# Rows of the first tile in ticks of their own, and every third of its first 48 added by TensorE

## The reference

```
q = (xf @ w_query).reshape(T, 8, 2, 128)
s = einsum('thcd,hckd->thck', q, sub_keys)
top_s, top_i = lax.top_k(s, 16)                 # of 128 keys, twice per head
cand_s, cand_i = sums and numbers of the 16 x 16 pairs
best_s, pos = lax.top_k(cand_s, 16)             # 16 experts of 16384 per head
gates = softmax(best_s)
a = gelu(einsum('cd,ced->ce', xc, expert_down[ic]))
out = einsum('ce,ced->cd', gates * a, expert_up[ic])
```

## Time and profile before

| | us |
|---|---|
| median of 3 runs | 1791.57 (1786.73 to 1792.23) |
| the profiled execution | 1788.6 |
| its span, first to last instruction | 1786.8 |
| busy in the span: PE, DVE, ACT, POOL | 1415.5, 1034.1, 439.6, 489.7 |
| DMA | 591.53 MB, mean 331 GB/s |

### The profile page before, as it was taken

How to read it: one execution, slowest core, us unless ns; L and a number is a source line. 1 busy time by engine, 2 the same in 40 slices (tenths; PEclk the granted TensorE clock), 3 DMA queues, 4 the chain that set the end, 5 groups by cost and what they waited for, 6 DMA issues and landing times. The chain is left out here.

```text
span 1786.8 us, 13852 instructions
## 1 busy us (share of the span) xinstructions
PE 1415.5 (79%) x4134; PEld 714.8 (40%) x4134; DVE 1034.1 (58%) x2185; ACT 439.6 (25%) x993; POOL 489.7 (27%) x498
## 2 busy tenths in 40 slices
PE   2998978798989999996968667698588676776665
PEld 2444445354444554443534333455233322222222
DVE  6654553653132223116587974997963467887875
ACT  2122313425224321011433131231012212211112
POOL 2101100210000000004236435554452354544441
PEclk8998998989999999998978779698799878888888
DMA  9978985976747777879879979999999699999995
GB/s 387 394 248 307 349 307 189 370 280 220 260 171 277 251 264 256 317 261 346 326 281 395 403 239 409 365 415 415 395 410 381 226 418 402 405 422 421 422 421 218
DMA packets 108941, 591.53 MB, mean 331 GB/s; under 512 B 12450, under 2 KB 12706, under 8 KB 60612
## 3 DMA queue, kind: packets, MB, share of 16 engines
q0 software_dynamic: 67776, 312.56, 44.7%
q1 hardware_dynamic: 41092, 278.10, 41.5%
HBM read 589.55 MB, written 1.05 MB: 331 GB/s over the span
## 5 line engine op out<-in xcount | busy, mean ns | idle before, releaser
L928 PE MATMUL bank<-ring,hT 128*128 128x512 f32 x1888 | 867.6, 615 | 44.1 <-DVE room L2009 12.0
L928 PEld LDWEIGHTS bank<-ring,hT 128*128 128x128 f32 x1888 | 366.2, 198 | 488.2 <-issue 451.1
L1168 PE MATMUL bank<-room 128*128 128x512 f32 x360 | 202.0, 713 | 90.2 <-ACT room L1458 74.6
L1757 DVE CUSTOM_DVE_ANT_0 room<-room 128x1024 f32<-128x1024 f32 x172 | 209.1, 1221 | 93.5 <-DMA room<-in_pair,idx 56.0
L859 POOL DMA_INDIRECT room<-in_peer_down,idx x84 | 91.9, 1094 | 514.8 <-DVE idx L1741 402.1
L1168 PEld LDWEIGHTS bank<-room 128*128 128x128 f32 x360 | 78.0, 228 | 211.1 <-ACT room L1458 110.4
L1772 DVE SCALAR_TENSOR_TENSOR x<-room,pcoef,x 128x1024 f32<-128x1024 f32 x113 | 145.3, 1286 | 27.0 <-DMA room<-in_peer_up,idx 23.6
L859 POOL DMA_INDIRECT room<-in_peer_up,idx x115 | 123.4, 1073 | 133.1 <-PE bank L1168 49.7
L907 PE MATMUL bank<-cst,room 128*128 128x128 f32 x424 | 65.7, 300 | 91.5 <-DVE room L1500 43.0
L859 POOL DMA_INDIRECT room<-in_pair,idx x88 | 100.9, 1147 | 111.6 <-PE bank L1168 51.7
L831 POOL DMA_DIRECT2D room<-in_w_mod x80 | 42.3, 530 | 318.1 <-DVE room L1527 199.8
(11 more groups left out here) (298 smaller groups left out, 1456.5 us busy)
## 6 DMA issues: line engine op xcount, KB each, us to landing
ring<-in_wpk SPq DMA_DIRECT2D x248, 1024.0 KB
room<-in_w_mod POOLq DMA_DIRECT2D x80, 512.0 KB
room<-in_w_mod SPq DMA_DIRECT2D x8, 1024.0 KB, 22.9
room<-in_norm_post_g POOLq DMA_DIRECT2D x4, 512.0 KB, 4.8
rowb<-in_gate_bias SPq DMA_DIRECT2D x4, 512.0 KB
room<-in_peer_up,idx POOLq DMA_INDIRECT x115
room<-in_pair,idx POOLq DMA_INDIRECT x88, 12.8
room<-in_peer_down,idx POOLq DMA_INDIRECT x84
```

What stands on the lines that cost most here:

```text
L928: last = mm(bank[p][:, :], lhs, ring[:, h % 4, k * N:(k + 1) * N], start=(kk == 0), stop=(h == halves[-1] and k == 3))
L1168: last = mm(bank[WORK[tile][i]][:, :], diag[:, nth % 4, :], row[:, i * N:(i + 1) * N], start=(v == mine[0]), stop=(v == mine[-1]), skip_gr ...
L1757: v.tensor_tensor_reduce(out=row, in0=row, in1=u_(k // MINE), scale=1.0, scalar=0.0, op0=ALU.mult, op1=ALU.add, accum_out=pa[:, k // TOPK ...
```

## The change

- A tick isn't a pick any longer. 18 ticks (REST) stand between tick 127 and the first pick of tile 1; `tick_of` and `pick_of` translate. In them only up rows of tile 0 are gathered and added. The first pair is asked for in tick 146, behind up row 127. There are 280 ticks instead of 262.
- `on_vector`: of rows 0 to 47 every third (u % 3 = 1, 16 rows) is added by PE; rows 48 to 111 by DVE; of rows 112 to 127 the even ones by PE. Tile 1 as before.
- LAG is 3 instead of 2.
- A spot's limit counts rows asked for (2 x most), so where a tick asks for one row it may take up to twice as many ticks.
- Row places: all ten that are free then are used to the end, and a place never used counts as used one tick before its birth, instead of coming first.
- Pair places are taken in one fixed cycle of 13.

```diff
-LAG = 2
-TICKS = PICKS + LEAD[1]
+LAG = 3
+REST = LEAD[0]
+TICKS = PICKS + REST + LEAD[1]
 def on_vector(u):
-    return u < 6 * TOPK or u % 4 == 3
+    return u % 3 != 1 if u < 3 * TOPK else u < 7 * TOPK or u % 4 == 3 or (u % 2 and u < MINE)
+def tick_of(g):
+    return g if g < MINE else g + REST
+def pick_of(k):
+    g = k if k < MINE else k - REST
+    return None if MINE <= k < MINE + REST or g >= PICKS else g
 def added_at(v):
-    return v + LEAD[v // MINE]
+    return tick_of(v) + LEAD[v // MINE]
-BORN = [0] * 9 + [9, 9] + [20, 20]
...
+PLACES = (4, 5, 6, 7, 8, 0, 1, 2, 3, 9, 10, 11, 12)
+PAIR = {g: (PLACES[(g - MINE) % len(PLACES)], (g - MINE) // len(PLACES)) for g in range(MINE, PICKS)}
+PAIR_LAST = {g: g - len(PLACES) for g in range(MINE + len(PLACES), PICKS)}
-    return (hh + 1) * TOPK if hh < PH else MINE + 1 if hh == PH else (hh - 1) * TOPK + 6
+    return (hh + 1) * TOPK if hh < PH else MINE + 1 if hh == PH else (hh - 1) * TOPK + REST + 6
     def spot(most):
         rows.add_due()
-        for _ in range(most):
-            target = start + (stop - start) * gone // whole
-            if asked(rows.at) < target:
-                rows.tick()
+        target, most = start + (stop - start) * gone // whole, asked(rows.at) + 2 * most
+        while asked(rows.at) < min(target, most):
+            rows.tick()
-        if rows.at == MINE + LEAD[0] + 8:
+        if rows.at == tick_of(MINE + 8):
             rows.add_through(MINE - 1)
             order.append(("final", 0))
-        _free = [s for s in PREFER if BORN_AT.get(s, 0) <= _k and not (s in ROWB and _k >= ROWB_ENDS)
-                 and (_k < MINE - 4 or 4 <= s < 8)]
-        _s = min(_free, key=lambda s: (SLOT_LAST[s][0], PREFER.index(s)) if s in SLOT_LAST else (-1, PREFER.index(s)))
+        _s = min((s for s in PREFER if BORN_AT.get(s, 0) <= _k and not (s in ROWB and _k >= ROWB_ENDS)),
+                 key=lambda s: (SLOT_LAST[s][0] if s in SLOT_LAST else BORN_AT.get(s, 0) - 1, PREFER.index(s)))
@@ POOL
                         elif p < 5:
                             pool.wait_ge(S("scm1"), 4)
+                            if p < 4:
+                                row_used(pool, SLOT_LAST[8 + p][1])
@@ ACT, DVE and POOL: g = pick_of(k) in place of k; choose, dots and groups go by g
```

More of the change, by code:

```diff
@@ L230 @@
 LEAD = (18, 6)
-LAG = 2
-TICKS = PICKS + LEAD[1]
+LAG = 3
+REST = LEAD[0]
+TICKS = PICKS + REST + LEAD[1]
 PIECES = [(L, third, k) for L in range(DEPTH) for third in range(3) for k in range(KC)]
 def on_vector(u):
-    return u < 6 * TOPK or u % 4 == 3
-def added_at(v):
-    return v + LEAD[v // MINE]
-BORN = [0] * 9 + [9, 9] + [20, 20]
[L247 to L255, removed]
+    return u % 3 != 1 if u < 3 * TOPK else u < 7 * TOPK or u % 4 == 3 or (u % 2 and u < MINE)
[4 more added lines that the diff above has]
+    return None if MINE <= k < MINE + REST or g >= PICKS else g
+def added_at(v):
+    return tick_of(v) + LEAD[v // MINE]
+PLACES = (4, 5, 6, 7, 8, 0, 1, 2, 3, 9, 10, 11, 12)
+PAIR = {g: (PLACES[(g - MINE) % len(PLACES)], (g - MINE) // len(PLACES)) for g in range(MINE, PICKS)}
+PAIR_LAST = {g: g - len(PLACES) for g in range(MINE + len(PLACES), PICKS)}
 ON_PE = sorted((u for u in range(PICKS) if not on_vector(u)), key=lambda u: (added_at(u), u))
@@ L259 @@
 DVE_NTH = {u: i for i, u in enumerate(ON_DVE)}
+ADDS = {added_at(v): [v] for v in range(PICKS)}
 def adds_of(k):
-    return [v for v in (k - LEAD[0], k - LEAD[1]) if 0 <= v < PICKS and added_at(v) == k]
+    return ADDS.get(k, [])
 def sums_at(hh):
-    return (hh + 1) * TOPK if hh < PH else MINE + 1 if hh == PH else (hh - 1) * TOPK + 6
+    return (hh + 1) * TOPK if hh < PH else MINE + 1 if hh == PH else (hh - 1) * TOPK + REST + 6
 EXP_NTH = {hh: i for i, hh in enumerate(sorted(range(T * PH), key=lambda hh: (sums_at(hh), hh)))}
@@ L274 @@
 GROUPS = [(hh * TOPK, TOPK) for hh in range(PH)] + [(MINE + 4 * m, 4) for m in range(MINE // 4)]
-GROUP_AT = {g + n: i for i, (g, n) in enumerate(GROUPS)}
+GROUP_AT = {tick_of(g + n - 1) + 1: i for i, (g, n) in enumerate(GROUPS)}
 def group_of(v):
@@ L322, in tick @@
             self.add_through(v - 4)
-        self.add_through(PAIR_LAST.get(self.at))
+        self.add_through(PAIR_LAST.get(pick_of(self.at)))
         for v in adds_of(self.at):
@@ L326, in tick @@
                 self.add_through(ON_PE[PE_NTH[v] - 4])
-        if self.at == MINE + BORN[-1]:
+        if self.at == tick_of(MINE + 9):
             self.add_through(MINE - 1)
@@ L449 @@
 ROW, ROW_LAST, SLOT_LAST, SLOT_USES = {}, {}, {}, [0] * 12
-for _k in range(MINE + LEAD[0]):
+for _k in range(MINE + REST):
     for _row in (("dn", _k), ("up", _k - LEAD[0])):
@@ L864, in _ @@
                 if step[0] == "tick":
-                    g, v = step[1], step[1] - LEAD[0]
-                    if g % TOPK == 0 and g < PICKS:
+                    g = pick_of(step[1])
+                    if g is not None and g % TOPK == 0:
                         pool.wait_ge(S("picked"), g // TOPK + 1)
-                    for kind, r in (("dn", g), ("up", v)):
+                    for kind, r in (("dn", step[1]), ("up", step[1] - LEAD[0])):
                         if not 0 <= r < MINE:
@@ L882, in _ @@
                         gather(row_at[i], "peer_down_2" if kind == "dn" else "peer_up_2", r).then_inc(row_in(i)[0], 16)
-                    if MINE <= g < PICKS:
+                    if g is not None and g >= MINE:
                         p, nth = PAIR[g]
@@ L1449, in _ @@
                         w, e = g // TOPK % 4, g % TOPK
-                        act.wait_ge(S("dn_used"), k)
+                        act.wait_ge(S("dn_used"), g + n)
                         af(pa[:, w, e:e + n], pa[:, w, e:e + n], ACT.Gelu).then_inc(S("gelu"), 1)
@@ L1753, in tick @@
             def tick(k):
-                if k < PICKS:
-                    row, landed, count = landed_row("dn", k)
+                g = pick_of(k)
+                if g is not None:
+                    row, landed, count = landed_row("dn", g)
                     dve.wait_ge(landed, count)
-                    v.tensor_tensor_reduce(out=row, in0=row, in1=u_(k // MINE), scale=1.0, scalar=0.0,
+                    v.tensor_tensor_reduce(out=row, in0=row, in1=u_(g // MINE), scale=1.0, scalar=0.0,
                                            op0=ALU.mult, op1=ALU.add,
-                                           accum_out=pa[:, k // TOPK % 4, k % TOPK:k % TOPK + 1]) \
+                                           accum_out=pa[:, g // TOPK % 4, g % TOPK:g % TOPK + 1]) \
                         .then_inc(S("dn_used"), 1)
@@ L1774, in tick @@
                             .then_inc(S("up_on_dve"), 1)
-                hh, e = k // TOPK, k % TOPK
+                if g is None:
+                    return
+                hh, e = g // TOPK, g % TOPK
                 if hh + 1 < T * PH and hh + 1 != PH and e in (2, 4, 6, 8):
```

## The result

The changed kernel takes 1779.13 us (median of 8, 1773.14 to 1786.64), the kernel before 1791.90 us (8 runs): the ratio is 0.9934 (0.9908 to 0.9959), so it is faster by 12.8 us. The forecast was 1768 us, a gain of 23 by its own sum. The time lies inside the range, but the gain is only about half of the one forecast. So I compare stretches, each from its own start. All times of the table are starts read from timelines of the profiled executions.

The account below looks back on a forecast made before the run. The second half was held bound by DMA bytes, with some 50 us idle in three stretches. 1788.6 - 15 (late) - 8 (early) = 1765.6 us, written as 1768 because the runs' median lies 3 us higher; range 1746 to 1791.

Parts of the forecast that it names:

- Bound: Second half, from 804 us: limited by bytes moved; some 50 us of idle DMA nearly all that can be won.
- the three stretches named: Idle DMA at 860 to 940 us (18.0 us), 1020 to 1080 us (14.1 us) and 1360 to 1420 us (18.2 us).
- Births and waits of POOL: First use of gateb's new places: POOL's waits of 12.0 and 19.6 us for post1 (DVE L1877) go.
- Pace: Behind quad_S(1,0): order runs three ticks ahead, moving six rows (7.5 us of DMA) from 1240 to 1340 us into the idle stretch from 860.
- Late part: From 1354 us to the first pair: last pair lands at 1741 instead of 1762.4 us; 15 us taken of 21 possible.
- a sign of failure beyond 1425 us: End of tile 0: the first pair asked for later than 1425 us would show the prediction wrong.
- somewhat under 18.2: Late hole: 15 us taken, below its 18.2 us of idle DMA, since DVE with 56 of 59 us had nothing to spare.
- Early part: 820 to 1110 us: 8 us gained, a quarter of the idle DMA; ends 32 us gained or 15 us lost.
- DVE's relief: 820 to 1110 us: DVE loses 20.6 us of adds and about a third of 14.9 us of waiting for up rows.
- PE's time: 820 to 1110 us: PE's 16 added adds take 28 to 57 us, against 40 us of idle PE.
- The slower rival: PE's early adds stand between the projections and delay them, 28 us on the path: 1802 us, chance 0.12.
- The clock paragraph: Adds moved to a stretch where PE's clock is cold would cost PE 57 us, not 28; no term used it.

Follow-up runs that it names:

- e1: The changed kernel with rows 0 to 47 of tile 0 all added by DVE, none by PE: 1745.49 us, 0.9734 of the kernel before.
- g1: e1 with the old rule for births, an unused place being taken first once born: 1760.96 us, 0.9840 of the kernel before.
- e4: The changed kernel with the old limit of a spot (3 ticks): 1790.85 us, 0.9997 of the kernel before.
- g2: e1 with the old limit of a spot (3 ticks): 1761.79 us, 0.9841 of the kernel before.
- e2: The changed kernel with the old choice of rows (PE adds 24 of rows 96 to 127, none of 0 to 47): 1758.79 us, 0.9805 of the kernel before.
- g4: e1 with rows taking only places 4 to 7 from tick 124 on: 1768.34 us, 0.9877 of the kernel before.
- f3: e1 plus only the hold: POOL reuses the 16 rows' places after PE passes the early adds' points: 1782.48 us, 0.9948 of the kernel before.
- h1: e1 with DVE's add of the 16 rows left out, a small memset in its place: 1746.53 us, 0.9743 of the kernel before.
- h2: e1 plus held places for the 16 rows and PE's two matmuls per row on constants: 1791.49 us, 0.9996 of the kernel before.
- f2: e1 plus two PE matmuls on constants, result unused, where each of the 16 early adds stood: 1756.09 us, 0.9802 of the kernel before.

## Why the prediction went wrong

**Bound.** Right. The second half is paid in idle DMA, in the three stretches named; e1 is 46 us faster than the kernel before, of the 50 us that the prediction held to be nearly all, and its gain over the changed kernel is about the DMA time that it fills.

**Births and waits of POOL.** Right in kind: DVE L1877 no longer appears in POOL's waits. I gave it no price of its own; it is worth 15.5 us (g1).

**Pace.** The direction was right, the size not given: 11.7 us after (e4), 16.3 us on e1 (g2). The reason, rows moved from a full stretch into an idle one ahead of 1340 us, explains only a part: in the profiles 8 and 6 us of it lie behind tile 1's last norm, where the ticks are the same again. What makes those is open; the births that move with the ticks are a candidate that no run tested.

**Late part.** The mechanism was right and the term too small. I took 15 of 21 us and measured 22.9, which needs both its causes: 14 us go without the moved adds (e2), and all of it without the ten places (g4). The first pair is asked for 24 us later than before by the clock (1437.4), which I had named as a sign of failure beyond 1425; it is 63.9 us behind the norm against 60.6 before, because the norm itself is late. The sign should have been measured from the norm. A share over 0.9 ahead of the first pair (0.93), no up row behind it and a tail of 24.4 us (1760.5 to 1784.9) came as written. The last pair landed only 1.9 us earlier by the clock, not 13 to 27, for the same reason. A share under 0.8 right behind choose(8) was a sign of being wrong; it came (0.79), and the late gain came all the same. The reason for "somewhat under 18.2" fell: DVE kept up, busy 46 of the 60 us ahead of the first pair and waiting for nothing but DMA.

**Early part: the step that failed.** It is the sentence "so POOL's lead of five or six ticks shrinks where PE's row is next; in 940 to 1020 us the DMA is full anyway", and the 8 us gained that followed. The lead doesn't shrink, it ends: POOL asks in order, so a kept place costs not one row but all rows behind it, and PE reaches the add only when what stands before it in its queue is through: POOL stood up to 23.0 us for one add. The forecast was 8 us gained; the profiles have 15.6 lost, the medians some 10. "No PE wait of 22 us in POOL before the first pair" failed three times over, while DVE waited no longer for PE (9.8 us against 10.0): it waited for rows. I had read the same thing in the earlier trace rows (22.5 us for PE's adds) as a fault of the query stage, and didn't carry it to the stage into which the adds were moved. Alone it costs 37.0 us on e1 (f3). "Full anyway" was true of before only; with POOL stopped the share fell to 0.93.

**DVE's relief.** I counted 20.6 us and a third of 14.9 as the gain's source. On e1 it is worth nothing that can be measured (h1), and at most 12.4 us where places are held (h2). DVE's busy share of 0.8 there was taken for a bound.

**PE's time.** The bounds were 28 to 57 us of work; the 16 adds took 36.7 us, nearer the warm end, and such work alone costs 10.6 us (f2). The slower rival had this mechanism at 28 us and so named the right engine with the wrong reason: its place in the queue cost more than its work. The clock paragraph held only in kind: both levels are there, 3.62 us for the early add at 920.2, behind waits of PE, and 1.88 us for the one at 930.6, behind a projection of 7.11 us; but 36.7 us for all 16 is far from the 57 of an always cold array.

**Sum.** Forecast: -15 late, -8 early. Profiles: -22.9 late, +15.6 early; the medians give -12.8 in all, so some +10 early. That the time fell into the range is luck: two terms were wrong, in opposite directions. Without PE's early rows the early part is -18.0 in the profiles, some -24 by the medians (-46.4 + 22.7).

## What to carry to other kernels

When work moves to another engine, count not only its duration but how long its buffer stays taken: until that engine's queue reaches it. Behind an in-order issuer of transfers one such buffer stops all the others, so a late consumer may want a buffer that no one else waits for (not tried here; taking the late consumer away was). And a busy engine isn't always a bound: leave out its work in one run before paying for its relief.

## What the runs showed of the hardware

Nothing new of the engines. What I had not expected is how far executions of this kernel differ ahead of any change: the first gather was issued between 814.2 and 822.0 us in the 16 profiled executions, though the work before it is the same; and the profiled execution can be the slowest or the fastest of its kernel (8.8 us above the median in e1, 8.4 below in g1). A comparison of two profiles is only good from a common event on, and a stretch that varies as much needs the medians beside it.
